# A one-core hybrid attention, retention and mixture-of-experts block: a ScalarE copy, an output product and a few VectorE operations issued at other places

## What is computed

```python
h = rmsnorm(x, norm_mix)
q_a, kv_a, g_a, q_r, k_r, v_r, g_r, gate_a, gate_r = split(h @ w_in)
y_a = nsa_attention(q_a, kv_a, sigmoid(g_a), ...)   # o_c + o_s + o_w, gated by head
#   o_c: softmax over 15 compressed blocks (p_c @ vc), o_s: selected blocks, o_w: window
y_r = retention(q_r, k_r, v_r, g_r, ret_norm)       # swish gate g_r times normed chunks
merged = sigmoid(gate_a) * (y_a @ w_nsa_up) + sigmoid(gate_r) * (y_r @ w_ret_up)
x = x + merged @ w_out
h = rmsnorm(x, norm_ffn)
x = x + hierarchical_moe(h, ...)                    # 32 experts, two for each token
out = rmsnorm(x, norm_final)
```

## Time and profile before

| | |
|---|---|
| median of 3 runs | 523.74 us (522.15 to 524.59) |
| the profiled execution, its own time | 523.5 us |
| its span (first to last instruction) | 521.3 us |
| TensorE busy | 477.5 us (92%), 2670 matmul records |
| VectorE busy | 176.3 us (34%) |
| ScalarE busy | 84.6 us (16%) |
| GpSimd busy | 39.4 us (8%) |
| bytes moved | 151.35 MB, mean 290 GB/s |
| mean granted TensorE clock | 0.96 of full |

### The profile page before, as it was taken

One profiled execution on the slowest core, in us unless ns is written; L12 is line 12 of the kernel. 1 busy time (PEld: TensorE's weight loads), 2 busy tenths in 40 slices (PEclk: granted clock), 3 DMA queues, 4 the chain that ended last, 5 costly groups with the idle time before them and its releaser, 6 DMA issues.

```text
span 521.3 us, 6638 instructions
## 1 busy us (share of the span) xinstructions
PE 477.5 (92%) x2670; PEld 301.7 (58%) x2670; DVE 176.3 (34%) x479; ACT 84.6 (16%) x234; POOL 39.4 (8%) x62
## 2 busy tenths in 40 slices
PE   5999999998599999999999989999999988969683
PEld 2599644553358888888684756365463525526231
DVE  1553039649261126202257453222131212122103
ACT  0000024221323000000001522121021201002012
POOL 0600050500000001000300300000000000000001
PEclk9999999999799999999999989999999987989968
DMA  8998769052007331899009999999999999999952
GB/s 272 405 372 222 248 245 395 9 221 102 0 21 303 124 138 60 318 419 392 1 29 395 373 356 417 417 428 431 408 431 416 422 427 412 428 409 431 415 214 85
DMA packets 20861, 151.35 MB, mean 290 GB/s; under 512 B 2947, under 2 KB 3396, under 8 KB 14172
## 3 DMA queue, kind: packets, MB, share of 16 engines
q1 hardware_dynamic: 19296, 147.88, 70.1%
q0 software_dynamic: 1296, 2.92, 2.7%
q10 hardware_dynamic: 236, 0.08, 0.1%
HBM read 148.25 MB, written 2.62 MB: 289 GB/s over the span
## 4 chain that ended last, share of the span: by engine, by line
PE 58%; DMA 27%; DVE 8%; issue 2%; SPq 2%; POOL 1%; ACT 0%; POOLq 0%; DVEq 0%; ACTq 0%
PE bank L642 39%; DMA ring<-in_moe_gate_up 16%; PE bank L666 10%; DMA bias_rows<-etab 8%; PE bank L1019 3%; PE bank L992 3%; DMA x<-in_x 2%; PE bank L672 2%; DMA Tb<-bias_rows 1%; SPq L431 1%; DVE nsa L1397 1%; DVE nsa L1538 1%; DVE ring L1491 0%; DVE ring L1479 0%; SPq L416 0%
## 5 line engine op out<-in xcount | busy, mean ns | idle before, releaser
L642 PE MATMUL bank<-hT_and_y,ring 128*128 128x256 f32 x384 | 84.3, 379 | 0.2 <-issue 0.2
L642 PEld LDWEIGHTS bank<-hT_and_y,ring 128*128 128x128 f32 x384 | 72.5, 190 | 10.5 <-DVE hT_and_y L1416 0.8
L1828 DVE COPY nsa<-bank 128x512 f32<-128x512 f32 x32 | 22.1, 691 | 96.1 <-PE bank L642 72.3
L642 PE MATMUL bank<-ring,nsa 128*32 128x512 f32 x336 | 43.9, 645 | 8.6 <-DMA ring<-in_moe_gate_up 8.5
L642 PEld LDWEIGHTS bank<-cst,nsa 128*128 128x128 f32 x256 | 33.9, 210 | 23.6 <-issue 18.3
L1331 ACT ACTIVATE nsa<-bank 128x512 f32<-128x512 f32 (+1 forms) x40 | 22.2, 554 | 135.9 <-PE bank L642 114.0
L642 PE MATMUL bank<-cst,nsa 128*128 128x32 f32 x256 | 36.6, 295 | 0.2 <-DVE nsa L1828 0.2
L1019 PE MATMUL bank<-nsa,Tb 128*128 128x128 f32 x256 | 32.9, 291 | 0.3 <-DVE nsa L1753 0.3
L1019 PEld LDWEIGHTS bank<-nsa,Tb 128*128 128x128 f32 x256 | 32.0, 206 | 0.4 <-issue 0.4
L992 PE MATMUL bank<-nsa 128*128 128x512 f32 x64 | 29.9, 607 | 0.8 <-ACT nsa L1331 0.8
L642 PE MATMUL bank<-Tb,ring 128*128 128x256 f32 x128 | 28.9, 379 | 0.0
(11 more groups left out here) (244 smaller groups left out, 616.7 us busy)
## 6 DMA issues: line engine op xcount, KB each, us to landing
ring<-in_moe_gate_up SPq DMA_DIRECT2D x21, 2048.0 KB, 20.0
ring<-in_dense SPq DMA_DIRECT2D x17, 2048.0 KB, 10.6
hT_and_y<-in_moe_gate_up SPq DMA_DIRECT2D x6, 2048.0 KB, 22.0
vr_and_gr<-in_moe_gate_up SPq DMA_DIRECT2D x5, 2048.0 KB, 22.5
windows<-in_moe_down SPq DMA_DIRECT2D x8, 512.0 KB, 20.7
qkT<-in_moe_down SPq DMA_DIRECT2D x8, 512.0 KB, 21.5
nsa<-in_moe_down SPq DMA_DIRECT2D x8, 512.0 KB, 20.5
keys<-in_moe_down SPq DMA_DIRECT2D x8, 512.0 KB, 19.4
```

What stands on the lines that cost most here:

```text
L642: return nc.tensor.matmul(o, l, r, start=s, stop=e)
L1828: V.tensor_copy(dst, bank[k][:, src]).then_inc(emptied[k], 1)
```

## The change

Five edits, of which none adds or removes an instruction:

- ScalarE: `copy("PcT")` stands now in front of `swish(0, 0)`, `exps(6)` and `exps(7)`, directly behind the exponential of the compressed scores.
- TensorE: the first product of `out` is made in front of `up6`, no longer of `up5`; VectorE's `first_weight_sum("out")` and `third_weight_sum("out")` follow one merge later.
- VectorE: the fourth left sum (`third_left_sum`, index 2) is made behind the other three, for `vr` and `gr` (from `hT`) and for `out`; in `out` it had stood before the merge of `up7`. TensorE's `outV` waits for three of the sums, and the product that reads index 2 for the fourth.
- VectorE, in `gr`: `seventh_product` stands between `scaled(6)` and `scaled(7)`, no longer behind both.

```diff
--- before.py
+++ after.py
@@ -906,7 +906,7 @@
             a11, a12, a21, a22 = left(gate[:, 0, :, :])
             b11, b12, b21, b22 = quarters("out")
             for i in range(KT):
-                if i == 5:
+                if i == 6:
                     oX = begin("outX")
                     for b in ("out0", "out1"):
                         pe.wait_ge(*loaded(b))
@@ -953,7 +953,7 @@
             pe.wait_ge(s_mrg, KT)
             done("outX", product(oX[:, :], a12, b21, False, True, range(3, 4)))
             oV = begin("outV")
-            pe.wait_ge(s_oS, 4)
+            pe.wait_ge(s_oS, 3)
             done("outV", product(oV[:, :], out_sums[:, 3], b22))
             oZ = begin("outZ")
             pe.wait_ge(s_T1, NTH["out"])
@@ -962,6 +962,7 @@
             pe.wait_ge(s_T2, NTH["out"])
             product(oW[:, :], out_sums[:, 1], b22, True, False).then_inc(s_P6, 1)
             stream_transposes("x2T00")
+            pe.wait_ge(s_oS, 4)
             pe.wait_ge(s_T3, NTH["out"])
             pe.wait_ge(s_P6_read, NTH["out"])
             product(oW[:, :], out_sums[:, 2], b12, False, False, range(2))
@@ -1223,11 +1224,11 @@
             act.wait_ge(s_cm, 1)
             pcf = Pc[:, :, :, :].rearrange("p t h c -> p (t h c)")
             nc.scalar.activation(pcf, pcf, ACT.Exp).then_inc(s_ce, 1)
+            o = take("PcT")
+            copy("PcT", PcT[:, :], o[:, 0:S])
             swish(0, 0)
             exps(6)
             exps(7)
-            o = take("PcT")
-            copy("PcT", PcT[:, :], o[:, 0:S])
             for pr in range(2):
                 o = take(f"PV{pr}")
                 copy(f"PV{pr}", yaT[:, pr, :], o[:, 0:S])
@@ -1457,9 +1458,9 @@
 
                 a11, a12, a21, a22 = left(v)
                 V.tensor_tensor(s[:, 0], a21, a22, ALU.add).then_inc(sums, 1)
+                dve.wait_ge(sums, 1)
+                V.tensor_tensor(s[:, 1], s[:, 0], a11, ALU.subtract).then_inc(sums, 1)
                 dve.wait_ge(sums, 2)
-                V.tensor_tensor(s[:, 1], s[:, 0], a11, ALU.subtract).then_inc(sums, 1)
-                dve.wait_ge(sums, 3)
                 V.tensor_tensor(s[:, 3], a12, s[:, 1], ALU.subtract).then_inc(sums, 1)
 
             def third_left_sum(v, s, sums):
@@ -1518,8 +1519,8 @@
             for i in range(1, 4):
                 dve.wait_ge(s_h, i)
             dve.wait_ge(*is_emptied("R"))
+            left_sums(hT, h_sums, s_S)
             third_left_sum(hT, h_sums, s_S)
-            left_sums(hT, h_sums, s_S)
 
             dve.wait_ge(s_sg, 1)
             link(tsc(sg[:, :, :], sg[:, :, :], 1.0, 0.5, ALU.add, ALU.mult))
@@ -1630,8 +1631,8 @@
             sixth_product("gr")
             fourth_weight_sum("gr")
             scaled(6)
+            seventh_product("gr")
             scaled(7)
-            seventh_product("gr")
             swish(0, 1)
             last_product("gr")
             swish(1, 1)
@@ -1679,15 +1680,13 @@
                 freed(f"up{i}", V.scalar_tensor_tensor(gate[:, 1, i, :], gate[:, 1, i, :], 1.0, o[:, S:2 * S], ALU.add, ALU.mult))
                 dve.wait_ge(*is_emptied(f"up{i}"))
                 V.tensor_tensor(gate[:, 0, i, :], gate[:, 0, i, :], gate[:, 1, i, :], ALU.add).then_inc(s_mrg, 1)
-                if i == 4:
+                if i == 5:
                     first_weight_sum("out")
-                if i == 5:
+                if i == 6:
                     third_weight_sum("out")
-                if i == 6:
-                    dve.wait_ge(s_mrg, 4)
-                    third_left_sum(gate[:, 0, :, :], out_sums, s_oS)
             dve.wait_ge(s_mrg, KT)
             left_sums(gate[:, 0, :, :], out_sums, s_oS)
+            third_left_sum(gate[:, 0, :, :], out_sums, s_oS)
 
             dve.wait_ge(s_rw, 64)
             V.tensor_tensor(wr[:, :, :], wr[:, :, :], vecT[:, KT:2 * KT].unsqueeze(2).broadcast_to((P, KT, NG + NE)), ALU.mult).then_inc(s_wr, 1)
```

## The result

The changed kernel takes 518.72 us (median of 20 runs, 516.88 to 522.68), the kernel before 522.82 us in as many runs beside it: ratio 0.9928, 95% interval 0.991 to 0.9945. On the 523.74 us of the start that is 520.0 us, against a forecast of 520.3. A second measurement on another occasion gave 518.93 against 522.12 us, ratio 0.9955 (0.9932 to 0.9977), which makes 521.4. So by the ratios the change is worth 2.4 to 3.8 us (1.2 to 4.7 with the intervals); the differences of the medians are 3.2 and 4.1. The ratios on record are not the quotients of the medians, which would be 0.9922 and 0.9939.

A forecast was written before the change was run, and what follows sets the result against it. TensorE up to `up7`, which releases a full stream of expert weights, was taken to bound the kernel. Terms 1.87 + 0.72 + 0.84 = 3.43 us off 523.5 gave 520.1, plus 0.24 for the median: 520.3 us, range 519.0 to 522.1.

The forecast's parts named there:

- Edit 1: Copy of PcT moved ahead on ScalarE: `attend(0)` starts at 133.97 instead of 135.84, once VectorE frees bank 3; 1.87 us.
- The clock's bounds: Copy's gain at `attend(0)`: 0.93 us if the clock rises no earlier than 138.48, 3.19 if TensorE returns at full clock.
- the rival that the clock comes back no earlier: Clock after `attend(0)` rises no earlier than before, so the copy gives 0.93 and the time is 521.2 us; chance 0.17.
- The signs of being wrong: Wait at `attend(0)` ending after 134.1, PEclk at 0.50 past 137, or SP's queue moving 3.4 us without the end.
- Edit 2: Seventh product of `gr` ahead of head 7's scaling: TensorE's wait at the last product goes; 0.72 us.
- Edit 3: First product of `out` one job later: TensorE's wait for `up4`'s merge to free bank 4 goes; 0.84 us, bounds 0 and 0.84.
- Edit 4: Fourth left sum behind the other three: no gain; in `out`, VectorE's extra 0.69 us is covered by 2.88 us of idleness.
- What TensorE wins before `up7` starts the stream earlier: The last 230 us are one full stream of expert weights released at `up7`; gains inside the stream are worth nothing.
- the rival of transfers that hide half: Stream at 371 GB/s from 272 to 312 us partly waits for release points; half of 3.43 lost, 522.0 us; chance 0.11.
- Low clock that holds on: `attend(0)` meets a 10.2 us stretch at 1.2 GHz, so the copy costs 1.91 us: 524.1 us; chance 0.04.
- The copy isn't waited for: TensorE before `attend(0)` does not wait for the copy of PcT, so moving it does nothing: 522.2 us; chance 0.03.
- the fourth sum on the path: VectorE binds behind `up7`, so the fourth left sum's 0.69 us lies on the path: 521.0 us; chance 0.06.

The follow-up runs named there:

- the start put off: The changed kernel with SP's loads of experts 1 to 3 held until `outV` is full: 519.03 against 522.11 us for the kernel before, ratio 0.9942.
- the later points put off: The changed kernel with TensorE multiplying `out3` five times instead of once, ahead of `out4` and later points: 522.95 against 522.12 us for the kernel before, ratio 1.0017.
- the norm row early: The changed kernel with the final norm's row load issued at 226 us, not at the stream's head: 517.47 against 522.11 us for the kernel before, ratio 0.993.

## Why the prediction was right, point by point

- **The views that were read.** That TensorE's path up to the stream is what counts held: the single gains read from it add up to that of the whole on the path, and the time fell by as much, within its interval. Of the single edits only the copy's gain is seen in the time itself.
- **Edit 1, 1.87 us.** Right in cause and size. 1.88 of the distances, 1.7 of the medians; the wait is 5.74 in place of 7.62, ended by the line named as late next, and moving that line gave the rest.
- **The clock's bounds, 0.93 and 3.19.** I took 2.64 us of low clock behind the restart to stay 2.64. It was 4.48 in the changed kernel and 3.40 with the copy alone, though in both the wait was 5.74. So the rival that the clock comes back no earlier held in these single executions: (4.48 - 2.64)/2 = 0.92 of that profile went to it, just the price given. But the three other executions with the old wait of 7.62 had 5.66 to 5.72, so 2.64 was the lucky one, not the rule. The mean of these four is 4.9 us behind the restart, that of six executions with the wait of 5.74 is 4.5 (2.9 to 6.0), so on average the gain isn't reduced, as far as so few tell. That the term came to 1.87 is right for a reason that the prediction did not have: it took one execution's 2.64 for the rule. In no run did the rise follow the restart at a fixed delay (2.6 to 6.0 us). The Trainium skill, "TensorE: Matmul & The Clock Gate", part 1, calls the activity watch free-running; the traces agree.
- **The signs of being wrong.** Two of the three named came up. The wait ended at 134.47, later than 134.1, but that is only the 0.50 by which the transposes came later: 134.47 - 0.50 is the 133.97 forecast. PEclk stayed at 0.50 past 137, to 138.95, and that is the clock's rival. Of what was to be seen, SP's norm loads stood at 269.27 and not 268.1: 3.43, less 0.92 for the clock and 0.50 for the transposes, and 0.3 more from edit 3, makes the 2.28 measured. The last weights came 1.28 us earlier and not 3.4.
- **Edit 2, 0.72 us.** Right: 0.71, and the transposes bind next, as said.
- **Edit 3, 0.84 us.** The cause was right, the term too small: 1.13. I gave the wait's own length as the upper bound. Where TensorE does not stop, a group of matmuls also starts before the one ahead has ended (the product at 269.08 starts while `up7`, 265.63 + 3.62 = 269.25, still counts as busy) and is itself shorter: 3.60 in the changed kernel, 3.70 behind the wait. That is 0.2 to 0.3 us that the idle column doesn't show.
- **Edit 4, 0.** Right: 0.04, and the cover is the gap before the second weight sum.
- **The sum, 3.43 us.** 3.70 of the distances; 3.8 and 2.4 of the two measurements. The profiled span fell by 4.1, and its nearness to the sum is partly chance: the stream's release moved by 2.28 alone, the last landing by 1.28, and the tail gave 2.8.
- **What failed: "What TensorE wins before `up7` starts the stream earlier".** The step says that the stream's start sets the end. It doesn't: put off by 7.1 us it cost nothing that the runs resolve (0.1 to 0.3 between medians), while the later points, put off by 6.1 us at `out4` and 4.5 at the first reload, cost 4.0. From the first reload (`hT_and_y`, line 431) to the last landing it takes 185.7 us before, 186.7 in the changed kernel, 186.5 with the start put off and 184.1 with the later points put off. In the other nine profiled executions it is 184.2 to 186.9, so differences of 2 us here are scatter. The end hangs on the points from `out4` on, that is, on when TensorE gets there. The number came out right only because the next sentence did hold: these points stand behind `up7` on the same engine and moved with it, by 2.28 us (`out4`) and 2.31 (first reload). The sign was in the earlier trace rows: 371 GB/s up to 312 us against 420 behind it is a stream with slack. The same slack answers the rival of transfers that hide half: they have room to start late, none once the reloads run. The time is also against it: the half-hidden 522.0 would be a ratio of 0.9967, outside the first interval, though inside the second.
- **Low clock that holds on.** It did hold on for 10.2 us in three executions, but in kernels with the old wait, where it costs 1.5 us; around the shorter wait it was 6.8 or 3.4. As a reason for a slower kernel it did not show. **The copy isn't waited for** and **the fourth sum on the path** fell with the runs of one edit.

## What to carry to other kernels

When an operation stands late in a queue, look for who is waiting behind it, then for what is late next, and price that too: here the copy gave 1.9 us, and the VectorE line that freed the bank gave some 7 more, of which 2.2 were the clock, which stayed up around a wait of 0.63 us. Of a long stream of loads, ask which release point is the last without slack: a stretch under the stream's later rate has room, and an earlier start there buys nothing. A wait can be worth a little more than its idle column says (1.13 for 0.84 with edit 3; edits 1 and 2 gave just what was read off), and the clock's share of one execution should be taken out before traces are compared.

## What the runs showed of the hardware

- **The clock.** Around a wait of 5.7 us it was low for 6.8 us in the changed kernel, with the copy alone, with the start put off, with the release points put off and with the norm row early, and for 3.4 us in the changed kernel's second measurement; around one of 7.6 us once for 6.8 and three times for 10.2; around one of 2.84 us for 3.4; around 0.63 us it didn't fall, in two kernels. That it also fell around a wait of 2.84 us, and only 0.2 us after TensorE was back, I had not expected.
- **The tail.** From the last gate-and-up weights to the end the same instructions took 22.7 to 25.8 us in different executions. Between the two profiles shown, 10 us at the low clock made 2.8 us and not 5, since at full clock TensorE waits for the last down weights instead.
- **GpSimd beside VectorE.** GpSimd's three additions on `x` should be alike. VectorE's weight sum with the first of them, and the last of them, in the changed kernel:

```profile
258.92 2.29 DVE L1475 TENSOR_TENSOR ring<-ring 128x2048 f32<-128x2048 f32 x1 [2.22 <-PE bank L666]
...
259.59 2.75 POOL L610 TENSOR_TENSOR x<-x,hidden_partial 128x512 f32<-128x512 f32 x1 [54.41 <-ACT hidden_partial L1191]
...
263.54 1.26 POOL L610 TENSOR_TENSOR x<-x,hidden_partial 128x512 f32<-128x512 f32 x1
```

The first took 2.75 us, the last 1.26. The first began while VectorE added two inputs that both lie in SBUF (258.92 to 261.21); VectorE kept its 2.29. The Trainium skill, "SBUF — State Buffer", in "Who interferes with whom", says that such an addition takes the read port that GpSimd shares; by that the first addition waited for it to end, at 261.21, and would then end at 262.47 (1.26 us later); it ended at 262.34, so the trace agrees, within 0.13 us. No run here moves the two apart, so the cause isn't shown.
